# A decoder step's input projection: the eight sample rows in four column groups of the array, folded by a constant matrix

## The reference

```
h = rmsnorm(x, norm_mix)                       # 1024 prompt rows, 8 sample rows
q, kc, vc, ks, vs, kw, vw, ng, dn_qkv, dn_a, dn_b, dn_z, mg_a, mg_b = split(h @ w_in)
```

## Time and profile before

| what | value |
|---|---|
| median of 3 runs | 2609.46 us (2608.59 to 2614.34) |
| the profiled execution, its own time | 2609.07 us |
| its span, first to last instruction | 2607.3 us |
| TensorE busy in the span | 2395.6 us (92%) |
| VectorE, ScalarE, GpSimd busy | 745.8, 487.2, 461.5 us |
| mean granted TensorE clock | 0.948 |
| projection block | from the start to about 443.5 us |

### The profile page before, as it was taken

How to read it: one execution, slowest core, us unless ns; L and a number is a source line. 1 busy time by engine, 2 the same in 40 slices (tenths; PEclk the granted TensorE clock), 3 DMA queues, 4 the chain that set the end, 5 groups by cost and what they waited for, 6 DMA issues and landing times. The chain is left out here.

```text
span 2607.3 us, 32747 instructions
## 1 busy us (share of the span) xinstructions
PE 2395.6 (92%) x12561; PEld 1449.0 (56%) x12561; DVE 745.8 (29%) x1524; ACT 487.2 (19%) x1331; POOL 461.5 (18%) x603
## 2 busy tenths in 40 slices
PE   8999998997879999699589999999499999999997
PEld 6446654886856656466466666544344444444443
DVE  2016342553556665344400000011411111111110
ACT  2101111332124555333100000010000000000000
POOL 1044121221311111200300000011112222222212
PEclk9999999998569999799789999999699999999999
DMA  5000300001300000465461000121579889889995
GB/s 171 33 32 33 128 12 1 2 2 38 66 1 2 1 2 1 121 180 158 126 178 33 2 31 33 51 92 62 216 271 317 315 314 314 315 317 321 317 318 160
DMA packets 185819, 331.66 MB, mean 127 GB/s; under 512 B 33989, under 2 KB 81614, under 8 KB 185486
## 3 DMA queue, kind: packets, MB, share of 16 engines
q1 hardware_dynamic: 161430, 293.38, 33.0%
q0 software_dynamic: 16096, 30.40, 4.2%
q10 hardware_dynamic: 8160, 6.07, 0.8%
HBM read 307.78 MB, written 51.37 MB: 138 GB/s over the span
## 5 line engine op out<-in xcount | busy, mean ns | idle before, releaser
L2535 PE MATMUL psum<-f_W,f_xT 128*128 128x512 f32 x1024 | 449.4, 597 | 6.1 <-DMA f_W<-w_up 4.6
L2535 PEld LDWEIGHTS psum<-f_W,f_xT 128*128 128x128 f32 x1024 | 192.8, 191 | 242.5 <-issue 231.7
L2044 PE MATMUL psum<-hT,x_wg 128*128 128x344 f32 x768 | 227.9, 455 | 4.4 <-DMA x_wg<-w_in 4.4
L2546 PE MATMUL psum<-f_W,f_aT 128*128 128x512 f32 x512 | 225.1, 593 | 1.1 <-DVE f_aT L2597 1.1
L379 PE MATMUL psum<-w,hT 128*128 128x512 f32 (+3 forms) x576 | 225.8, 550 | 0.0
L2044 PEld LDWEIGHTS psum<-hT,x_wg 128*128 128x128 f32 x768 | 146.8, 191 | 81.2 <-DMA x_wg<-w_in 4.5
L379 PE MATMUL psum<-hT,w 128*128 128x344 f32 x576 | 168.9, 454 | 0.0
L379 PEld LDWEIGHTS psum<-w,hT 128*128 128x128 f32 (+1 forms) x576 | 102.5, 181 | 114.3 <-issue 107.9
L2546 PEld LDWEIGHTS psum<-f_W,f_aT 128*128 128x128 f32 x512 | 94.8, 190 | 108.5 <-issue 107.1
L2586 DVE TENSOR_TENSOR f_a<-f_sg,psum 128x512 f32<-128x512 f32 x32 | 22.0, 687 | 443.7 <-ACT f_sg L2566 443.7
L1581 ACT ACTIVATE a_P<-psum,a_nmax 128x512 f32<-128x512 f32 (+4 forms) x256 | 122.8, 493 | 125.1 <-DVE a_nmax L1499 84.8
(11 more groups left out here) (506 smaller groups left out, 3241.7 us busy)
## 6 DMA issues: line engine op xcount, KB each, us to landing
f_W<-w_gate SPq DMA_DIRECT2D x32, 2048.0 KB, 14.8
f_W<-w_up SPq DMA_DIRECT2D x32, 2048.0 KB, 20.9
f_W<-w_down SPq DMA_DIRECT2D x32, 2048.0 KB, 9.6
k_stage<-cache_nsa SPq DMA_DIRECT2D x128, 192.0 KB, 2.5
w<-w_in SPq DMA_DIRECT2D x6, 2048.0 KB, 8.0
x_wg<-w_in SPq DMA_DIRECT2D x8, 1024.0 KB, 11.4
x<-x_prompt SPq DMA_DIRECT2D x8, 512.0 KB, 5.6
o_w<-w_out SPq DMA_DIRECT2D x2, 2048.0 KB
```

The costliest lines, as they stand in the source:

```text
L2044: ins = nc.tensor.matmul(PS[b + i][:, 0:n], wg[q % 3][:, k, i, c:c + P], hT[:, k, t0:t0 + n], start=(k == 0), stop=(k == KD - 1))
L2535: ins = nc.tensor.matmul(PS[bank][:, :], xT[par][:, k, :], w[par][:, k, :], start=(k == 0), stop=(k == KD - 1))
L2546: ins = nc.tensor.matmul(PS[5 + half][:, :], aT[:, k, :], wd[par][:, k, 512 * half:512 * half + 512], start=(k == 0), stop=(k == 3))
```

## The change

The sample unit takes 32 weight columns instead of 8 (tokens 1000 to 1031, of which the last 8 are the samples) and puts the product of contraction piece k at PSUM partitions 32 \* (k % 4). Pieces 0 to 3 start four groups of partitions, and pieces 4 to 7 add to them. The bank then holds four partial sums, with the samples in partitions 24 to 31 of each group. ScalarE copies all 128 partitions into a new tile `parts`. A product with a new constant matrix `fold` (128x8, ones where the partition modulo 32 is 24 + s) adds the four partial sums for each sample, into bank 7 (the first three) or 6 (the last), one unit later on TensorE. ScalarE copies that to where the sample rows stood before. Those who read the sample rows, or use bank 7 or 6 next, wait for this second copy (`fold_copied`). In load 6 the sample unit becomes the first of the nine instead of the last.

```diff
--- before.py
+++ after.py
@@ -68,6 +68,7 @@
     put("ident", np.eye(P))
     put("mhalf", np.full((P, 16), -0.5))
     put("ones", np.ones((P, P)))
+    put("fold", (i[:, None] % 32 == 24 + np.arange(TS)[None, :]) * 1.0)
     put("tri", (i[:, None] <= i[None, :]) * 1.0)
     put("strictT", (i[:, None] < i[None, :]) * 1.0)
     put("upper", np.where(i[None, :] >= i[:, None], BIG, 0.0))
@@ -207,6 +208,7 @@
         par_loaded, gain_loaded, act_step, dve_step, qsq_done, qss_done, mean_done, r_done, gain_ready, x_done, xg_done, rope_done, stored = map(
             sem, ("par_loaded", "gain_loaded", "act_step", "dve_step", "qsq", "qss", "mean", "r", "gain", "x", "xg", "rope", "stored"))
         x_loaded = [sem(f"x_loaded{i}") for i in range(4)]
+        folded, fold_copied = map(sem, ("folded", "fold_copied"))
         head_loaded, table_loaded, ng_loaded, squares_done, msq_done, rs_ready, xn_ready, turned, ht_done = map(
             sem, ("head_loaded", "table_loaded", "ng_loaded", "squares", "msq", "rs", "xn", "turned", "ht"))
         N = Region(L, A_DN, A_OA)
@@ -226,6 +228,7 @@
         par, y, z = F("decay_par", [P, 8]), F("decay_y", [P, NT, 4]), F("decay_z", [P, NT, 4])
         taps = F("conv_taps", [P, NC, NR])
         sq = F("q_sq", [P, 2, 12, HD])
+        parts = F("sample_parts", [P, 512])
         tail = L.at("conv_tail", A_RS, [P, NC * P])[32:43, :]
 
         loads = [([(1024, QKV0), (AB0, Z0)], 1024), ([(0, 512)], 0), ([(512, 1024)], 512)]
@@ -236,7 +239,7 @@
             width = sum(b - a for a, b in pieces)
             first.append(len(units))
             if at is not None:
-                for t in range(NT + 1):
+                for t in (range(NT + 1) if c < 6 else (NT, *range(NT))):
                     n = P if t < NT else TS
                     dst = R[:, t, at:at + width] if t < NT else Rs[0:TS, at:at + width]
                     if at == 0:
@@ -247,6 +250,7 @@
                     for t0, n in THIRDS:
                         units.append((c, P, n, m, t0, dnT[:, 4 * (c - 3) + m, t0:t0 + n]))
         ends = first[1:] + [len(units)]
+        sample_units = [i for i, unit in enumerate(units) if unit[1] == TS]
         counts, done = [], [0, 0]
         for c, (pieces, _) in enumerate(loads):
             done[c % 2] += 16 * len(pieces)
@@ -321,6 +325,7 @@
 
             def last_rows(j):
                 pe.wait_ge(act_copied, ends[DN + j])
+                pe.wait_ge(fold_copied, 3)
                 if j:
                     pe.wait_ge(tail_copied, j)
                 for x in range(4):
@@ -338,6 +343,7 @@
                 c, j, t0, n = norms[u]
                 if u == 0:
                     pe.wait_ge(root_done, 2)
+                    pe.wait_ge(fold_copied, 4)
                 if u >= 2:
                     pe.wait_ge(unit_done, u - 1)
                 out = PS[5 + u % 2]
@@ -358,6 +364,15 @@
                     ins = nc.tensor.transpose(PS[4 + 2 * (t % 2) + k // 4][:, (k % 4) * P:(k % 4) * P + n],
                                               xn[0:n, t % 2, k * P:(k + 1) * P], C["ident"][0:n, 0:n])
                 ins.then_inc(turned, 1)
+
+            def fold(x):
+                width = units[sample_units[x]][2]
+                if x == 0:
+                    pe.wait_ge(table_loaded, 16)
+                pe.wait_ge(act_copied, sample_units[x] + 1)
+                if x:
+                    pe.wait_ge(fold_copied, x)
+                nc.tensor.matmul(PS[7 if x < 3 else 6][0:TS, 0:width], C["fold"], parts[:, 0:width], start=True, stop=True).then_inc(folded, 1)
 
             pe.wait_ge(head_loaded, 16)
             turn(0)
@@ -372,6 +387,10 @@
                 if i >= 4:
                     pe.wait_ge(act_copied, i - 3)
                 for k in range(KD):
+                    if m_rows == TS:
+                        q = 32 * (k % 4)
+                        ins = nc.tensor.matmul(PS[i % 4][q:q + 32, 0:n], hT[:, k, TT - 32:TT], w[c % 2][:, k, 0:n], start=(k < 4), stop=(k >= 4))
+                        continue
                     if m is None:
                         lhsT, rhs = hT[:, k, t * P:t * P + m_rows], w[c % 2][:, k, 0:n]
                     else:
@@ -380,6 +399,8 @@
                 ins.then_inc(mm_done, 1)
                 if i < NT - 1:
                     turn(i + 2)
+                if i - 1 in sample_units:
+                    fold(sample_units.index(i - 1))
                 if i == NT + 1:
                     pe.wait_ge(table_loaded, 16)
                     rows_of_taps()
@@ -419,9 +440,21 @@
             for i, (c, m_rows, n, m, t, dst) in enumerate(units):
                 act.wait_ge(mm_done, i + 1)
                 s = PS[i % 4][0:m_rows, 0:n]
-                if c == 1:
+                if i in sample_units:
+                    s, dst = PS[i % 4][:, 0:n], parts[:, 0:n]
+                    if sample_units.index(i):
+                        act.wait_ge(folded, sample_units.index(i))
+                elif c == 1:
                     s = s.rearrange("p (g j d) -> p g j d", g=NKV, d=HD)
                 nc.scalar.copy(dst, s).then_inc(act_copied, 1)
+                if i - 1 in sample_units:
+                    x = sample_units.index(i - 1)
+                    _, _, width, _, _, out = units[i - 1]
+                    act.wait_ge(folded, x + 1)
+                    s = PS[7 if x < 3 else 6][0:TS, 0:width]
+                    if x == 1:
+                        s = s.rearrange("p (g j d) -> p g j d", g=NKV, d=HD)
+                    nc.scalar.copy(out, s).then_inc(fold_copied, 1)
                 if i + 5 <= NT:
                     square(i + 5)
                 if i == ends[0] + 1:
@@ -441,7 +474,10 @@
                 pool.wait_ge(msq_done, t + 1)
                 pool.tensor_tensor(rs[0:n, t:t + 1], rms[0:n, t:t + 1], C["mhalf"][0:n, 0:1], ALU.pow).then_inc(rs_ready, 1)
             for c, n, x in cases:
-                pool.wait_ge(act_copied, first[2] + c + 1)
+                if c < NT:
+                    pool.wait_ge(act_copied, first[2] + c + 1)
+                else:
+                    pool.wait_ge(fold_copied, 3)
                 if c >= 2:
                     pool.wait_ge(qss_done, c - 1)
                 for at, h, slot in GROUPS:
@@ -491,6 +527,7 @@
             def decay_steps():
                 dve.wait_ge(par_loaded, 32)
                 dve.wait_ge(act_copied, ends[0])
+                dve.wait_ge(fold_copied, 1)
                 for i, (n, t, a, b, out) in enumerate(decays):
                     yy, zz = y[0:n, 0:t], z[0:n, 0:t]
                     step(nc.vector.tensor_tensor(yy, a, par[0:n, 4:8].unsqueeze(1).to_broadcast([n, t, 4]), ALU.add))
```

## The result

| | median | runs | lowest to highest |
|---|---|---|---|
| before, timed with the changed kernel | 2610.40 us | 8 | 2608.59 to 2615.57 |
| changed | 2596.14 us | 8 | 2592.80 to 2604.47 |

What follows compares the result with a forecast made beforehand. TensorE was taken to bound the projection (428.28 of 443.5 us). Gains of 2.3 + 8.0 + 3.8 + 0.1 = 14.2 us off 2609.07 gave 2594.9, 2595.3 from the median, stated as 2595; range 2590 to 2602.

Steps and rivals of the forecast that it cites:

- Four groups at once: Sample units: four column groups run at once as at line 1934, 1.72 us instead of 6.87, 0.97 instead of 3.89.
- Place by place: Projection: net gains of 2.3 us in load 0, 8.0 in loads 1 and 2, 3.8 in load 6, 0.1 at the end.
- What hides the rest: ScalarE's extra copies and fold waits are covered; the q and k squares lose 4.7 us of cover, at no cost.
- The stop of 3.04 us moves along: Load 6: TensorE's wait for GpSimd's powers hangs on `last_rows(2)`, so the idle 3 us stays and everything moves together.
- Exposed weight loads: Rival at the sample units: none of 64 weight loads hides, costing 5.8 to 8.7 us, time 2601 to 2604; chance 8%.
- the slower case: Rival at the sample units: groups wait for each other, four folds add 4.1 us, less 0.1, 2613.5; chance 4%.

Runs made afterwards that it cites:

- one-group kernel: The changed kernel with all eight pieces of a sample unit in one column group, same folds, copies and load 6 order: 2615.58 us against 2612.57 for the kernel before.
- the combination: The changed kernel with folds in four column groups, `last_rows(2)` right behind load 6's sample unit, and `block_out`'s two sample units in four groups with fold: 2584.34 us.
- those of `block_out`: The changed kernel with the output projection's two sample units in four column groups, folded behind the transposes of tile 7: 2587.63 us alone.

## Why the prediction was right

- *Four groups at once, read from line 1934.* It held with 512 moving and 32 weight columns: factors of 1.9 with two groups and 3.7 with four in busy time, and 1.33 us from the first to the last start of 16 instructions (1.92 less 0.59), which is three distances of a set of four.
- *Place by place*: load 0 gave 2.3 us (11.04 to 8.75 from the sample unit to the conv rows; forecast 2.3), loads 1 and 2 4.0 each (4.0), load 6 3.8 (3.8). 14.1 with the 0.1 at the end, against 14.2. That the medians give 14.3 as well is in part luck, since their interval is 11.0 to 16.7 us.
- *What hides the rest.* The squares of the sample rows:

```profile
172.72 1.74 POOL L484 TENSOR_TENSOR q_sq<-Rs 8x512 f32<-8x512 f32 x3 [5.87 <-ACT Rs L457]
```

  7.0 us sooner than the earlier trace rows, of which 1.4 are the earlier start of this execution: 5.6, as worked out. VectorE's idle time before the copy of the tail fell from 7.65 to 4.08, where 3 to 4 were forecast:

```profile
232.92 0.68 DVE L584 COPY conv_tail<-psum 11x512 f32<-11x512 f32 x1 [4.08 <-PE psum L332]
```

- *The stop of 3.04 us moves along*: shown, and shown by what moves it (`last_rows(2)` sooner). That run also shows a second condition, which the prediction didn't say: once `last_rows(2)` is out of the way the chain hangs on the sums of head 7, and the powers came only 3.7 us sooner.
- *The rivals.* Exposed weight loads: refuted by the 32- against 8-column run, and by the unit's length. By the Trainium skill ("TensorE: Matmul & The Clock Gate", Part 3, "What overlaps and what doesn't") these loads should not overlap, as all four groups have the same rows; the trace has 16 loads of 109 ns within a unit of 1.85 us at no cost. What the slower case would cost is what the one-group kernel measures: +3.4 us where +4 was forecast. The Trainium skill ("TensorE: Matmul & The Clock Gate", Part 3, "Measured speedup vs the span model") has its factor of 3.07 for four row tiles of 32 contraction rows, and none for four column groups; here four column groups gave 3.7.
- *A slip without effect.* The prediction calls `parts` the weights of the fold. By the form 128\*8 with 288 or 512 moving columns the weights are the constant matrix, and `parts` moves. The price of 2 x 0.243 and 2 x 0.429 us was worked out from the moving columns, so the sum stands.
- *What wasn't foreseen* is how the two profiled spans differ by 16.2 us rather than 14.1: 1.4 from an earlier start, 2.2 from behind the projection (2163.3 to 2161.2 us from the next block's first product to the end), less 1.5 for the slow clock after the stop. These are differences between executions, and the medians differ by 14.3.

## What to carry to other kernels

Where a matrix product has few rows (at most 32 here, in float32) and a long contraction, put pieces of the contraction into four column groups of the array and add the four partial sums with a constant product: the time falls to about a quarter plus one fold, and a neighbour in the same kernel that already runs so gives the rate. Price the fold as streams on the path, cut it into four groups as well, and look where a full unit of other work can stand between the copy and the fold. When such a product stands ahead of a chain that other engines run, count to the instruction that starts the chain.

## What the runs showed of the hardware that was not expected

The granted clock fell to half (1.2 GHz) in a stretch in which TensorE was never idle. In the kernel with `last_rows(2)` sooner (us, TensorE busy, loads, VectorE, ScalarE, GpSimd, clock):

```profile
359.60:361.60 2.00, 2.00 (x19) 1.96 (x18) 0.00 (x0) 1.54 (x2) 0.00 (x0) 1.00 0.00 0
361.60:366.90 5.30, 5.30 (x11) 2.27 (x10) 5.07 (x9) 0.00 (x0) 4.81 (x1) 0.68 0.00 0
366.90:370.30 3.40, 3.40 (x10) 1.49 (x9) 3.29 (x4) 0.00 (x0) 3.40 (x1) 1.00 0.00 0
```

What stood before the fall were the sums of head 7, 18 matmuls with one moving column each, at full busy share, and then the first instructions of a full unit, still at 1.00 (361.6 to 363.0 us). What made it fall is not shown. The same sums stand ahead of these two units in every kernel here. In the kernel with the fold in four groups the clock fell behind them too (0.57 from 359.3 to 361.2 us). In the combination, with the order of `last_rows(2)` sooner, no fall followed them, and in the changed kernel the clock stayed at 1.00 from 358.8 to 375.2 us, across them and the two units behind. There the fall came after the 3.04 us stop instead and lasted longer than before (0.73 here, 0.84 in the earlier trace rows):

```profile
378.10:390.90 12.80, 11.68 (x30) 5.88 (x31) 3.19 (x5) 0.00 (x0) 0.08 (x1) 0.73 0.00 1
```

The unit behind the stop took 9.51 us in this execution of the changed kernel and 8.02 in its other profiled one, 8.06 before, and 7.03 at full clock, by this alone. So such a spell cost the unit 1.0 to 2.5 us here, and nothing where it fell ahead of the stop (the fold in four groups). In the combination no slow spell fell into the projection. These spells explain a part of why single runs of one kernel differ. Behind the projection, where the code is the same in all runs but those of `block_out`, executions lasted between 2161.2 and 2168.7 us; the longest had the lower granted clock (0.93 against 0.94), and why it was lower was not looked into.
